# A head's output norm issued in the next head's score stage, in a two-block transformer kernel

## The reference, cut to what matters

```python
def diff_attention(q, k, v, q_g, k_g, rel_bias, lam, subln_g, lambda_init):
    q = rmsnorm(q, q_g); k = rmsnorm(k, k_g)
    ...
        logits = logits + bias[None, :, None]
        p = jax.nn.softmax(logits, axis=-1)
        attn = p[:, :, 0] - lam * p[:, :, 1]
        return jnp.einsum('bhqk,bkhe->bqhe', attn.astype(v.dtype), v)
    ...
    out = rmsnorm(out, subln_g) * (1.0 - lambda_init)
```

## Time and profile before

| | us |
|---|---|
| Median of 3 runs (2057.5 to 2059.64) | 2058.53 |
| Profiled execution, its own time | 2057.48 |
| Its span | 2055.7 |
| PE busy | 1951.7 (95%) |
| DVE busy | 1080.3 (53%) |
| POOL busy | 1237.3 (60%) |
| ACT busy | 501.0 (24%) |

### The profile page before, as it was taken

How to read it: one execution, slowest core, us unless ns; L and a number is a source line. 1 busy time by engine, 2 the same in 40 slices (tenths; PEclk the granted TensorE clock), 3 DMA queues, 4 the chain that set the end, 5 groups by cost and what they waited for, 6 DMA issues and landing times.

```text
span 2055.7 us, 23472 instructions
## 1 busy us (share of the span) xinstructions
PE 1951.7 (95%) x9015; PEld 1598.3 (78%) x9015; DVE 1080.3 (53%) x1516; ACT 501.0 (24%) x1001; POOL 1237.3 (60%) x1018
## 2 busy tenths in 40 slices
PE   6888887999999999999999999999999899999997
PEld 4666666888888888888878777888778788888886
DVE  7666657999355231226876686333555473223134
ACT  4444443333122010112133333010222221001012
POOL 6233325788776776766633444676767567677662
PEclk8999998999999999999999999999999999999998
DMA  5122112333333333333322322333433233333321
GB/s 158 47 62 62 49 34 75 89 89 113 103 93 92 103 92 97 98 94 101 93 52 52 77 62 67 103 93 92 123 93 103 75 100 93 98 96 94 102 78 56
DMA packets 341169, 177.39 MB, mean 86 GB/s; under 512 B 14453, under 2 KB 338203, under 8 KB 341060
## 3 DMA queue, kind: packets, MB, share of 16 engines
q1 hardware_dynamic: 339044, 173.28, 29.3%
q10 hardware_dynamic: 2016, 2.62, 0.6%
HBM read 173.75 MB, written 2.13 MB: 86 GB/s over the span
## 4 chain that ended last, share of the span: by engine, by line
PE 74%; DVE 20%; ACT 3%; issue 3%; DMA 0%; ACTq 0%; SPq 0%; DVEq 0%
PE bank L649 21%; PE bank L653 21%; PE bank L651 21%; PE bank L767 2%; PE bank L744 1%; DVE aPR L1613 1%; PE bank L715 1%; DVE fPR L1878 1%; DVE aPR L1615 1%; DVE IT L1713 1%; DVE XC L1694 1%; DVE HS L1723 1%; DVE HS L1724 1%; DVE aPR L1605 1%; PE bank L733 1%
## 5 line engine op out<-in xcount | busy, mean ns | idle before, releaser
L618 POOL TENSOR_TENSOR WL<-RAW,WH 128x1024 fp32r<-128x1024 f32 (+3 forms) x331 | 813.1, 2457 | 27.7
L649 PE MATMUL bank<-HH,WH 128*128 128x512 f32 x1560 | 623.2, 399 | 9.3 <-DVE SQ L1573 7.4
L653 PE MATMUL bank<-HH,WL 128*128 128x512 f32 x1560 | 618.8, 397 | 0.0
L651 PE MATMUL bank<-HL,WH 128*128 128x512 f32 x1560 | 615.6, 395 | 0.0
L614 POOL TENSOR_TENSOR gate<-gate 128x1 f32<-128x1 f32 x331 | 86.6, 262 | 758.8 <-PE bank L653 710.3
L649 PEld LDWEIGHTS bank<-HH,WH 128*128 128x128 f32 x1560 | 296.0, 190 | 75.1 <-issue 16.8
L615 POOL TENSOR_SCALAR WH<-RAW 128x1024 fp32r<-128x1024 f32 (+3 forms) x331 | 342.8, 1036 | 0.9 <-issue 0.2
L653 PEld LDWEIGHTS bank<-HH,WL 128*128 128x128 f32 x1560 | 296.0, 190 | 60.4 <-issue 1.7
L651 PEld LDWEIGHTS bank<-HL,WH 128*128 128x128 f32 x1560 | 296.1, 190 | 60.2 <-issue 3.4
L1764 DVE TENSOR_TENSOR X<-X,bank 128x512 f32<-128x512 f32 x80 | 55.0, 687 | 200.6 <-PE bank L653 200.6
L1486 DVE SCALAR_TENSOR_TENSOR HL<-X,PARAM,HH 128x512 fp32r<-128x512 f32 x40 | 90.8, 2269 | 30.0 <-ACT HH L1091 30.0
(11 more groups left out here) (397 smaller groups left out, 3188.0 us busy)
## 6 DMA issues: line engine op xcount, KB each, us to landing
RAW<-in_w_in SPq DMA_DIRECT2D x107, 512.0 KB, 3.7
RAW<-in_w_up SPq DMA_DIRECT2D x32, 512.0 KB, 3.9
RAW<-in_w_down SPq DMA_DIRECT2D x32, 512.0 KB, 3.9
RAW<-in_w_ffn_gate SPq DMA_DIRECT2D x22, 512.0 KB, 3.6
RAW<-in_w_ffn_up SPq DMA_DIRECT2D x22, 512.0 KB, 3.7
RAW<-in_w_xkv SPq DMA_DIRECT2D x16, 512.0 KB, 3.8
RAW<-in_w_ffn_down SPq DMA_DIRECT2D x16, 512.0 KB, 3.5
RAW<-in_w_proj_attn SPq DMA_DIRECT2D x8, 512.0 KB, 3.9
```

Source lines behind the costliest of these rows:

```text
L618: nc.gpsimd.tensor_tensor(WL[:, s, 0:k, :], RAW[:, s, 0:k, :], WH[:, s, 0:k, :].bitcast(F32), ALU.subtract).then_inc(S_[f"unit_cut{s}"], 1)
L649: mm(psum[s][:, 0:n], WH[:, s, k, :], hi(k), start=(k == 0), stop=False)
L651: mm(psum[s][:, 0:n], WH[:, s, k, :], lo(k), start=False, stop=False)
L653: last = mm(psum[s][:, 0:n], WL[:, s, k, :], hi(k), start=False, stop=(k == tiles - 1))
```

## The change

The output norm of head h (for h = 0 to 6) is issued inside head h+1. ACT's square stays at the end of head h. PE's sum of squares goes behind the 5 steps of block t = 1 of head h+1; ACT's Ln and Exp go behind its exponential t = 2, and its high half behind exponential t = 4; DVE's scaling goes behind the taking of the next q product (query block 1), and its low half behind the combining of query block 1, in the turn of query block 2. The counts that the waits compare with are changed to the new order. The last head's own norm stays at its end. No instruction of an engine is added or taken out, no tile or bank is added.

```diff
--- before.py
+++ after.py
@@ -747,7 +747,7 @@
                 if n == J - 1:
                     last.then_inc(S_[tag + "_pv"], 1)
 
-            def attend(tag, M, kind, h, steps, share, add_bias=None, stats=None):
+            def attend(tag, M, kind, h, steps, share, add_bias=None, stats=None, late=None):
 
 
 
@@ -773,6 +773,8 @@
                     run(steps, share[0])
                     if t == 0 and kind is not KIND_SWA:
                         v_transpose(tag, M, h)
+                    if t == 1 and late:
+                        late()
                 run(steps, share[1])
                 pe.wait_ge(S_[tag + ("_exp" if kind is KIND_FOX else "_row_max")], h * 8 + 8)
                 transpose_probs(tag, M, kind, h, 0)
@@ -820,9 +822,15 @@
                 steps = chain(from_h("first", 0, 0), from_h("first", 0, 1)) if last else \
                     chain(*[from_h("qkv", h + 1, j) for j in range(3)])
                 attend("a", M1, KIND1, h, steps, (2, 8, 8, 3) if last else (5, 10, 10, 2),
-                       stats=None if last else lambda side: qk_stat1(h + 1, 3 * h + 2, side))
+                       stats=None if last else lambda side: qk_stat1(h + 1, 3 * h + 2, side),
+                       late=(lambda: out_stat1(h - 1, 3 * h + 1)) if h else None)
+                if last:
+                    out_stat1(h, 3 * h + 2)
+
+            def out_stat1(h, n):
+
                 pe.wait_ge(S_["a_o_sq"], h + 1)
-                stat("a", 3 * h + (2 if last else 4), ones[:], M1["SQ"][:, 2, :])
+                stat("a", n, ones[:], M1["SQ"][:, 2, :])
 
             for h in range(0, HEADS - 1):
                 head1(h, False)
@@ -1175,7 +1183,15 @@
                     A(M1["VH"][:, 0], OUTB[:].rearrange("p (j e) -> p j e", j=NB), ACT.Copy
                       ).then_inc(S_["a_v_hi"], 1)
 
-                exps("a", M1, KIND1, h, v_hi, None if last else lambda t: square1(h + 1, 0) if t == 5 else None)
+                def after(t):
+                    if t == 2 and h:
+                        rsqrt_stat("a", 3 * h + 1, 1.0 / P, M1["RQ"][:, 2, :])
+                    if t == 4 and h:
+                        out_hi1(h - 1)
+                    if t == 5 and not last:
+                        square1(h + 1, 0)
+
+                exps("a", M1, KIND1, h, v_hi, after)
                 if not last:
                     if h + 2 < HEADS:
                         load_bias1(h + 2)
@@ -1189,7 +1205,11 @@
                         qk_hi1(h + 1, n - 2)
                 act.wait_ge(S_["a_out_taken"], h + 2)
                 A(M1["SQ"][:, 2, :], M1["OR"][:], ACT.Square).then_inc(S_["a_o_sq"], 1)
-                rsqrt_stat("a", 3 * h + (2 if last else 4), 1.0 / P, M1["RQ"][:, 2, :])
+                if last:
+                    rsqrt_stat("a", 3 * h + 2, 1.0 / P, M1["RQ"][:, 2, :])
+                    out_hi1(h)
+
+            def out_hi1(h):
                 act.wait_ge(S_["a_o_norm"], h + 1)
                 A(AO[0][:, bass.ds(h, 1), :], M1["OR"][:].unsqueeze(1), ACT.Copy).then_inc(S_["a_o_hi"], 1)
 
@@ -1650,6 +1670,10 @@
                 def between(i):
                     if i == 1 and not last:
                         take_qk1(h + 1, 0)
+                    if i == 1 and h:
+                        out_norm1(h - 1, 3 * h + 2)
+                    if i == 2 and h:
+                        out_lo1(h - 1)
 
                 def row_max1(t, part, i, bank):
                     return biased_max(M1, KIND1, t, part, i, bank, falling(BIAS1[:, h % 2, :], P * (i + 1)), 3e38)
@@ -1669,10 +1693,17 @@
                 V.tensor_copy(M1["OR"][:], OUTB[:]).then_inc(S_["a_out_taken"], 1)
                 if not last:
                     take("qkv", h + 1, 2, scaled(M1["VR"][:]))
-                dve.wait_ge(S_["a_stat_read"], 3 * h + (3 if last else 5))
-                dve.wait_ge(S_["a_o_sq"], h + 1)
+                if last:
+                    out_norm1(h, 3 * h + 3)
+                    out_lo1(h)
+
+            def out_norm1(h, n):
+
+                dve.wait_ge(S_["a_stat_read"], n)
                 V.scalar_tensor_tensor(M1["OR"][:], M1["OR"][:], small[:, SUBL:SUBL + 1], M1["RQ"][:, 2, :],
                                        ALU.mult, ALU.mult).then_inc(S_["a_o_norm"], 1)
+
+            def out_lo1(h):
                 dve.wait_ge(S_["a_o_norm"], h + 1)
                 dve.wait_ge(S_["a_o_hi"], h + 1)
                 V.tensor_tensor(AO[1][:, bass.ds(h, 1), :], M1["OR"][:].unsqueeze(1),
```

## The result

| | us |
|---|---|
| Median after, 4 runs (2046.0 to 2048.29) | 2047.62 |
| Median before, beside them | 2058.02 |
| Ratio, 95% interval | 0.9949 [0.9932, 0.9966] |
| Profiled execution after, own time (its span) | 2047.36 (2045.5) |

The change makes the kernel faster by 10.4 us, half a per cent. The forecast was 2044.8, with a range from 2037.5 to 2052.

A forecast was written before the change was run, and what follows sets the result against it. PE, 95% busy, was taken as the bound, with gains only where it waits on DVE and the norm. Heads 1 to 6 (8.7) plus head 7 (5.0) gave 13.7 us off 2057.48: 2043.8, as a median 2044.8; range 2037.5 to 2052.

The forecast's parts named there:

- PE at the head's start: Three PE gaps, before the sum of squares and in the first scores, go: 2.17 us until the q product's end.
- ACT at nothing: Moved Ln, Exp and high half on ACT delay nothing that matters: cost 0, bounds 0 and 1.4 us per head.
- DVE's scaling: Behind taking q it meets POOL's WH cut, ends 0.54 us after it; PE keeps 1.55 of 2.2, waiting about 0.7.
- The other price: Skill page's lock: blocked scaling starts about 115 ns after WH, ends near 130.1; each head gains 0.3 us less.
- Low half, row maximum t = 6, last add: Later score stage: row maximum 1.33 us earlier, last add over WH ending 0.54 after it; a head gains 1.45.
- the 1.55 of the bound: Upper end of the gain forecast per head, 1.35 to 1.55 us, with 1.45 taken.
- Head 7: Last head, paced by DVE: gains 3.7 us, up to 7.0 if PE's clock stays at 2.4 GHz; 5.0 taken.
- the case named against it: Last head: first unit's cut meets two instructions of the last combining; WL before the add gives back 2.4 us.
- DVE first at the last combining: Rival, 20%: the last add takes its turn before WH, ends 2.15 us earlier than before; total 2038.6.
- The wait only moves: Rival, 8%: scores or combining wait anew; heads 1 to 6 give nothing, head 7 gives 3.7; total 2054.8.
- Slower: the last add behind WL: Rival, 5%: query block 3's add waits for all of WL, ending 1.1 us later than before; 12.5 slower, 2071.
- It decides from a shift of 1.0 us on.: Margin of the slower rival: DVE's chain must come 1.0 us later against PE for the add to fall behind WL.

The follow-up runs named there:

- the repeat: The changed kernel measured a second time with no edit: 2046.0 us, ratio 0.9943.
- e2: Changed kernel with PE's sum of squares and ACT's root back at the head's end, only high half, scaling and low half moved: 2050.3 us, ratio 0.9964.
- e3: Changed kernel with only PE's sum of squares moved; ACT's root and high half, DVE's scaling and low half back at the head's end: 2077.33 us, ratio 1.0097.
- e6: Changed kernel with POOL's cut started by the k product (head 7: first unit's cut) waiting for the last combining: 2036.62 us, ratio 0.9894.
- e9: Kernel before the change, with POOL's cut started by the k product waiting for the last combining: 2051.56 us, ratio 0.9971.
- e1: Changed kernel with DVE's scaling of the last head's output ahead of taking q instead of behind it: 2067.49 us, ratio 1.0044.
- e8: Changed kernel with POOL's q cut waiting for the last combining and its k cut for the output copy, head 7's first-unit cut also held: 2029.18 us, ratio 0.9857.

## Why the prediction was right, and where it was not

**Direction, mechanism and size** came out: the stretch of the heads gave 14.06 us, in the repeat 13.29, for 13.7 in the sum. That the sum came so near is in part luck: heads 1 to 6 gave 1.0 us more than forecast (9.68 for 8.7), and head 7 gave 0.6 less, in the repeat 1.5 less. Going through the steps:

*PE at the head's start.* Forecast 2.17 us until the end of the q product; taking q comes 9.74 us after the output copy (127.74 - 118.00) for 12.23, so 2.49 earlier. The 0.32 more is a cost of a stop that I hadn't counted, shown in the last section.

*ACT at nothing* held. Exponential t = 4 stood idle 3.70 us before its row maximum came, with the moved root well in front of it.

*DVE's scaling* took 1.25 us (forecast "about 1.2") and ended 0.53 after WH (forecast 0.54). The other price, from the Trainium skill's page SBUF — State Buffer, would have put its end at 129.07 + 0.12 + 0.75 = 129.9; the trace has 129.60. The row was right. The page gives its 115 ns for a wait until the end of a DVE instruction; here it is DVE that waits for POOL. PE's new wait before scores t = 6 is listed with 0.52 us, which is 0.68 in the issue of matmuls (forecast 0.7).

*Low half, row maximum t = 6, last add.* Counted from the output copy, the row maximum t = 6 starts 1.58 us earlier (forecast 1.33), the last add ends 1.60 earlier (19.84 for 21.44). The add met WH as forecast, with 0.02 us between their starts. A head gained 1.60 to 1.62 for 1.45 forecast, just above the 1.55 of the bound: PE's and POOL's extra 0.3 us came through.

*Which part gives what.* e2 splits the 1.60 into 0.86 (DVE's place) and 0.74 (PE's place), and e3 shows that PE's part is a loss unless DVE's work goes too. The prediction had the idle times before both, but didn't say that one without the other would cost.

*Head 7.* Forecast 5.0 between 3.7 and 7; measured 4.38 and 3.49, the second just under the lower bound. The clock in the scores was regained, as hoped (1.00 from 268 to 279). But the case named against it came true as well: the first unit's cut met both instructions of the last combining (1.35 and 2.71 us on DVE), PE waited 4.51 us, and the clock fell behind it:

```profile
279.18 1.35 DVE L1633 TENSOR_SCALAR aPR<-aPR,RS,small 128x512 f32<-128x512 f32 x1
280.57 2.71 DVE L1635 SCALAR_TENSOR_TENSOR aPR<-aPR,RS 128x512 f32<-128x512 f32 x1
```

```profile
283.42 1.73 PE L733 MATMUL bank<-ident,aPR 128*128 128x128 f32 x7 [4.51 <-DVE aPR L1635]
```

e6 holds that cut and has head 7 at 21.95: the long wait and the low clock behind it are worth 4.1 us.

*From the stretch to the total.* Of 14.06 us in the heads, 10.4 were left in the first measurement. In the profiled execution the rest of the span is 1841.2 us against 1837.3 before; in the repeat it is 1838.5, and in the other kernels, none of which touches that part, 1836.7 to 1840.7. A part of it may lie in cross attention. The same window of after, and then of before (the repeat has 0.97 there); as after runs some 10 us ahead there, the two don't hold quite the same work:

```profile
1600.00:1650.00 50.00, 45.89 (x233) 38.84 (x231) 28.99 (x39) 13.87 (x27) 27.82 (x22) 0.93 0.26 75
```

```profile
1600.00:1650.00 50.00, 44.20 (x261) 38.69 (x260) 28.51 (x46) 13.79 (x29) 27.81 (x23) 1.00 0.27 77
```

Another part stands ahead of head 0's output copy, 88.20 in after, 86.51 before, 86.89 in the repeat. The scatter is 4 us, about what the total lost. Whether some 2 us of it belong to the change was not settled. The two kernels with the old order, before and e9, have the smallest rest of all (1837.3 and 1836.7), but their profiled executions were also 1.0 and 3.7 us faster than their medians, so this decides nothing.

**The rivals.** *DVE first at the last combining* did not happen: with 0.02 us between the starts, POOL won here, as it did with 0.01 before. But these hundredths are not the margin. POOL's tiny instruction L614, which comes directly before WH, started 0.28 us ahead of the add (136.01 against 136.29), and in e3 the add is listed before WH and waits all the same, with L614 0.12 ahead of it. No run has an add ahead of L614, so what would happen then is open; by the prediction's own times (136.47 against 137.63 - 1.55 = 136.08 for L614, which starts at 137.63 in the kernel before) it was 0.4 us away and not 0.2. *The wait only moves* did not happen. *Slower: the last add behind WL* did not happen in the change, but e1 is that case, and it shows **the one wrong step: "It decides from a shift of 1.0 us on."** I measured the distance from the add's issue to the end of WH. What decides in these runs is whether the cut begins before the scaling ahead of the add: then that scaling waits, and WL comes in front of the add. In after, that scaling begins at 135.71, 0.56 us before WH at 136.27. These 0.56 are only the scaling's own 0.55, at whose end WH starts; the cut as a whole began with L614 at 136.01, 0.30 after the scaling. In e1 L614 is 0.19 ahead of the scaling (139.97 against 140.16), in head 7 of after 0.12 ahead (279.06 against 279.18), and in both the add waits for WL; in every head where L614 came 0.30 or more behind the scaling, the add waited for WH alone. So the margin was between 0.30 and 0.42 us, less than half of what I gave, and e1 used it up: against the scaling it brought L614 forward by 0.49. I had watched for DVE coming late; what came was POOL coming early, set off by a PE that no longer waited. The price of 1.1 + 1.6 = 2.7 us a head looks right against 2.66 measured, but that is luck, for its parts are not: the add ended where it did before, not 1.1 later, and what is lost lies behind it, where the clock is low (0.90 over the head for 1.00).

## What to carry to other kernels

Work whose result is needed late belongs where the engine would wait anyway, on every engine of its chain at once: the sum of squares alone on PE's side cost 3 us a head, with DVE's part moved it gained. When an order of two engines hangs on a few tenths of a microsecond, settle it with a semaphore and don't hope: holding one cut on the engine that has time (POOL, 61% busy) was worth 9 us, and holding two was worth 17, more than the 10.4 to 12.5 of the reordering itself. And after an edit look for the next meeting downstream, since an edit that removed a 0.5 us stall (e1) cost 21 us.

## What the runs showed of the hardware that was not expected

**A stop costs PE a tenth of a microsecond beyond the wait.** Scores of 256 columns before and after the change, the first one behind a wait and the same one without. Before:

```profile
124.95 0.39 PE L767 MATMUL bank<-aQH 128*128 128x256 f32 x1 [1.05 <-DVE NMAX L1605]
125.18 0.28 PE L767 MATMUL bank<-aQL,aQH 128*128 128x256 f32 x1
```

After:

```profile
124.57 0.28 PE L767 MATMUL bank<-aQH 128*128 128x256 f32 x1
124.69 0.28 PE L767 MATMUL bank<-aQL,aQH 128*128 128x256 f32 x1
```

The next matmul starts 0.23 us later in the one, 0.12 in the other. The second stop shows the same (126.90, the next at 127.12), and so does the third: the pair of matmuls for the sum of squares takes 1.12 us behind its wait and 1.02 in after, without one. Together these three stops make the 0.3 us by which PE came earlier than forecast.

**Which of DVE and POOL has its turn next hangs on a few tenths of a microsecond.** The same pair of instructions of the last combining took 0.55 + 1.55 us in after and 1.29 + 2.70 in e1; in head 7 of after 1.35 + 2.71. In these runs, a DVE scaling that waited for WH was followed by WL before the add had its turn; one that came before the cut left only WH in front of the add. POOL pays too: WL took 2.69 and 2.71 us where DVE's instruction had its turn between WH and WL, and 2.39 where WL came first. e6 and e8 show that the meeting is the cause: with the cut held the pair takes 0.55 + 0.75 in every head. That it is L614, and not WH, whose start counts fits all heads of all runs, but no run moved it alone.

**The low clock follows a long wait.** Behind the wait of 4.06 us in e1 the granted clock was 0.50 (1.2 GHz) from 144.30 to 147.50; in the heads of after, with a wait of 1.7 us at the same place, it stays 1.00. How long it stays low is not fixed by the wait: in e3 PE waited 3.9 us in each of two heads that follow each other, and the clock was back at 0.93 in the window from 134 to 136 us, 3 to 5 us behind the first wait, while behind the second it was 0.50 from 166 to 170 and 0.55 from 170 to 172. That is the head of 35.82 us.
